# The sample cache on 128 partitions instead of 127, and four weight tiles queued later at the start

## The chip, the cores and the metric

The kernel runs on all 8 cores of one Trainium2 chip, each with its own part of the work and with no exchange between them. The time is that of the slowest core, in microseconds (us). The engines are named as in the profile: PE (TensorE, matmuls; PEld its weight loads), DVE (VectorE), ACT (ScalarE), POOL (GpSimd) and SP (SyncE, which here issues DMAs only). Each engine runs its own instructions strictly in the order in which they were written; semaphores join the engines.

## The reference

One inference step of a two-layer decoder trunk of width 1024, for 4 prompts of 4096 rows and for 128 samples of one row each. Layer 0 is a mixer with two halves (sliding-window attention over 128 positions with 8 heads, 2 key/value heads of 64, a relative-position bias and a sink; and a chunked gating network), layer 1 a gated recurrence. After each comes a feed-forward network of width 2816 with a residual.

What matters here is the attention of the samples. Each sample has a cache of the last 128 keys and values, and one new key and value:

```
k_all = concat(cache_k, k_new)                     # 129 positions
bias  = -inf where (distance < 0) or (distance >= 128), else rel_bias[bucket(distance)]
o     = softmax(q k_all / 8 + bias, with the sink) v_all
new_k_sample = k_all[1:]                           # the last 128 positions
```

The oldest cached row lies at distance 128, outside the window: it takes no part in the attention, and it is not in the returned cache either. So 127 of the 128 cached rows are used.

## The kernel before

A core has 18 blocks of 128 prompt rows and 16 samples. The blocks form four groups, A (blocks 0 to 3), B (4 to 8), C (9 to 12 and the samples) and D (13 to 17). Each group passes through layer 0's mixer (`l0`), its feed-forward network (`f0`), layer 1's mixer (`l1`) and its network (`f1`). The plan pairs them in nine phases, so that a mixer of one group runs beside a network of another; the samples' attention falls into phase 4, where `l0` of group C runs beside `f1` of group B.

The order of the work is not written by hand. Each operation is recorded with what it reads and writes, and a planner (`Sched`) gives every engine one fixed list. An operation's due time is its place in its phase, by the matmul time recorded before it, minus its `lead`. A DMA that opens a buffer, or that waits for nothing, is held back until the matmuls have come within 0.15 of its due time. The planner's costs decide the order only; at run time the lists are followed as they stand.

Two queues carry the loads. POOL issues the weights (`load_w`, L620: tiles of 128 x 2048, from fp32 to bf16 on the way, 512 KB as written), into 6 buffers `wm` for the mixers and 4 buffers `wf` for the networks. SP issues everything else. In the program's first phase POOL begins with six `wm` tiles: `kv`, `q0`, `q1`, `u0`, `u1`, `g0`. SP begins with a gain, a table, four blocks of rows (`X<-xin`, 512 KB each) and then small constants, `qkn` among them.

The samples' cache comes in four groups of four samples (`cache_group`, L849 on). For each group SP loads four samples' keys and then their values (L852) into fp32 tiles `p` of 127 partitions x 4 x 128: one cached row on each partition. ACT or POOL casts each tile to bf16 (L596), PE transposes the keys (L861), ACT or DVE copies the result, and the scores and sums follow later (`sample_group`). That is eight loads of 254 KB. In the traces such a tile is called `p`, as is every tile of that pool; `p<-ck` and `p<-cv` are the loads. Between the fourth and the fifth stands the load of a table, `gain<-lnr` (L1280).

The returned cache is moved by two copies in DRAM, `nks<-ck` and `nvs<-cv` (L1324), issued much earlier, and a store of the new row.

Of the kernel before, what the change touches and what calls it, by code (L numbers as in the profile page):

```python
# [9 lines left out]
ALU = mybir.AluOpType  # L10
AF = mybir.ActivationFunctionType
# [343 lines left out]
NS = 16  # L355
# [46 lines left out]
def _t5_bucket_np(dist):  # L402
    d = np.maximum(dist, 0)
    dl = np.maximum(d, 1).astype(np.float32)
    val = (np.log(dl / np.float32(16)) / np.float32(math.log(128 / 16)) * np.float32(16)).astype(np.float32)
    large = 16 + val.astype(np.int32)
    large = np.minimum(large, 31)
    return np.where(d < 16, d, large)


def build_consts():
    ohA = np.zeros((33, 384), np.float32)
    for j in range(384):
        dist = j - 128
        if 0 <= dist < 128:
            ohA[int(_t5_bucket_np(np.array(dist))), j] = 1.0
        else:
            ohA[32, j] = 1.0
    ohS = np.zeros((33, 128), np.float32)
    for j in range(128):  # L420
        ohS[int(_t5_bucket_np(np.array(127 - j))), j] = 1.0
    return ohA, ohS


# [59 lines left out]
def build_program(NG, WIDX):  # L484
    nc = bass.Bass("TRN2", target_bir_lowering=False)
    din = lambda name, shape: nc.dram_tensor(name, list(shape), F32, kind="ExternalInput").ap()
    dout = lambda name, shape: nc.dram_tensor(name, list(shape), F32, kind="ExternalOutput").ap()
    xin = din("xin", [NTOK + NS, D])
    ck_d = din("ck", [NS, 127, 128])
    cv_d = din("cv", [NS, 127, 128])  # L490
    sin_d = din("sin", [NS, 8, 128, 128])
    wall = din("wall", [NG, 128, 2048])
    par_d = din("par", [128, 22])
# [29 lines left out]
    with es:  # L523
        S = Sched()
        nsem = [0]

        def mksem():
            nsem[0] += 1
            return Sem(es.enter_context(nc.semaphore("d%d" % nsem[0])))

        def sb(name, shape, dt):
            return es.enter_context(nc.sbuf_tensor(name, list(shape), dt))

        def mkpool(name, n, size, dt, dma=False, **kw):
            t = sb(name, [128, n, size], dt)
            return Pool(name, [t[:, i, :] for i in range(n)], [mksem() for _ in range(n)] if dma else None, **kw)
# [3 lines left out]
        pWM = mkpool("wm", 6, 2048, BF16, dma=True, fifo=True, margin=0.4)  # L540
# [15 lines left out]
        identB = sb("identB", [128, 128], BF16)  # L556
# [4 lines left out]
        onesB = sb("onesB", [128, 64], BF16)  # L561
# [11 lines left out]
        biasS = sb("biasS", [128, 8], F32)  # L573
# [15 lines left out]
        def ra(st, bl, half):  # L589
            return [r_aT[(st.col[b] // 128, half)] for b in bl]  # L590
# [4 lines left out]
        def cp(e, out, in_):  # L595
            return e.copy(out=out, in_=in_) if CUR[0] == "act" else e.tensor_copy(out=out, in_=in_)  # L596
# [15 lines left out]
        outs = []  # L612
# [20 lines left out]
        r_id, r_mk, r_v1, r_par, r_rel, r_qn, r_ws, r_bs, r_bs0, r_bs1, r_ab, r_tab, r_es, r_pp, r_qk = [Buf("c%d" % i) for i in range(15)]  # L633
# [116 lines left out]
        def l0(st):  # L750
            g0 = load_gain(nrm_d[0])
            w_kv = load_w(pWM, "kv")
            w_q = [load_w(pWM, "q%d" % k) for k in range(2)]
            w_u = [load_w(pWM, "u%d" % c) for c in range(2)]
            w_g = [load_w(pWM, "g%d" % c) for c in range(2)]
            allb = st.kv + ([SB] if st.samples else [])
            norm(st, allb, g0)
            qT = {}
# [87 lines left out]
            def cache_group(q):  # L846
                n4 = slice(4 * q, 4 * q + 4)
                c3 = lambda ap: ap.rearrange("p (n f) -> p n f", n=4)
                cast = []  # L849
                for src in (ck_d, cv_d):  # L850
                    f = p25.get("cache", 2)
                    S.op("sp", lambda e, f=f, src=src: e.dma_start(out=c3(f.ap[0:127, 0:512]), in_=src[n4].rearrange("n j f -> j n f")), w=[f], dma=f, nbytes=1 << 19, lead=0.2)  # L852
                    c = p12.get("cacheb")
                    S.op(("act", "pool"), lambda e, f=f, c=c: cp(e, c.ap[0:127, 0:512], f.ap[0:127, 0:512]), r=[f], w=[c])
                    cast.append(c)
                kb, vb = cast
                kts, bt = p12.get("kts"), bank()

                def tr(e):
                    for j in range(4):  # L860
                        i = e.transpose(bt.bf[:, j * 128:j * 128 + 127], kb.ap[0:127, j * 128:(j + 1) * 128], identB[0:127, 0:127])  # L861
                    return i
                S.op("pe", tr, r=[kb, r_id], w=[bt])
                S.op(ANY, lambda e: cp(e, c3(kts.ap[:, 0:512])[:, :, 0:127], c3(bt.bf[:, 0:512])[:, :, 0:127]), r=[bt], w=[kts])
                return kts, vb

            def sample_group(kts, vb, vn, pd, qt, qp, q):
                bs = bank()

                def sc(e):  # L870
                    for j in range(4):
                        i = e.matmul(bs.ap[0:127, j * 8:(j + 1) * 8], lhsT=kts.ap[:, j * 128:j * 128 + 127], rhs=qp()[:, 4 * q + j, :], start=True, stop=True)
                    return i
                S.op("pe", sc, r=[kts, qt], w=[bs])
                f = p25.get("attS")
                S.op("dve", lambda e: e.tensor_tensor(out=f.ap[0:127, 0:32].rearrange("p (n h) -> p n h", n=4), in0=bs.ap[0:127, 0:32].rearrange("p (n h) -> p n h", n=4),
                                                      in1=biasS[0:127].unsqueeze(1).broadcast_to([127, 4, 8]), op=ALU.add), r=[bs, r_tab], w=[f])
                S.op("act", lambda e: e.activation(out=qt.ap[0:127, 128 + 32 * q:160 + 32 * q], in_=f.ap[0:127, 0:32], func=AF.Exp), r=[f], w=[qt])
                pt = lambda: qt.ap[0:127, 128 + 32 * q:160 + 32 * q].rearrange("p (n h) -> p n h", n=4)
                p3 = lambda: pd.ap[0:NS, 0:128].rearrange("p (n h) -> p n h", n=NS)  # L880
                bo = bank()

                def pv(e):
                    for g in range(2):
                        o = bo.ap[g * 64:(g + 1) * 64, 0:16]
                        for j in range(4):
                            e.matmul(o[:, j * 4:(j + 1) * 4], lhsT=vb.ap[0:127, j * 128 + g * 64:j * 128 + g * 64 + 64], rhs=pt()[:, j, 4 * g:4 * g + 4], start=(j == 0), stop=False, skip_group_check=True)
                        e.matmul(o.rearrange("p (n h) -> p n h", n=4), lhsT=vn.ap[0:NS, 128 + g * 64:192 + g * 64], rhs=p3()[:, 4 * q:4 * q + 4, 4 * g:4 * g + 4], start=False, stop=True, skip_group_check=True)
                    for g in range(2):
                        o = bo.ap[g * 64:(g + 1) * 64, 64:80].rearrange("p (n h) -> p n h", n=4)  # L890
                        e.matmul(o, lhsT=onesB[0:127, :], rhs=pt()[:, :, 4 * g:4 * g + 4], start=True, stop=False)
                        e.matmul(o, lhsT=onesB[0:NS, :], rhs=p3()[:, 4 * q:4 * q + 4, 4 * g:4 * g + 4], start=False, stop=False)
                        i = e.matmul(o, lhsT=onesB[0:1, :], rhs=es8[0:1, 4 * g:4 * g + 4].unsqueeze(1).broadcast_to([1, 4, 4]), start=False, stop=True)
                    return i
                S.op("pe", pv, r=[vb, vn, pd, qt, r_es, r_mk], w=[bo])
                S.op("dve", lambda e: e.reciprocal(out=f.ap[:, 32:48], in_=bo.ap[:, 64:80]), r=[bo], w=[f])
                c0 = st.sl(SB).start + 4 * q
                S.op("dve", lambda e: e.tensor_tensor(out=aTm[:, 0:4, c0:c0 + 4], in0=bo.ap[:, 0:16].rearrange("p (n c) -> p c n", c=4), in1=f.ap[:, 32:48].rearrange("p (n c) -> p c n", c=4), op=ALU.mult),
                     r=[bo, f], w=ra(st, [SB], 0))
# [383 lines left out]
        def at(phase, s):  # L1283
            S.key = (phase, s)
            stream[0] = s
# [35 lines left out]
                    ffn(st, int(what[1]), st.body if what == "f0" else st.out, 1 if what == "f0" else 3)  # L1321
        at(3, 0)
        for dst, src in ((nks_d, ck_d), (nvs_d, cv_d)):
            outs.append(S.op("sp", lambda e, dst=dst, src=src: e.dma_start(out=dst[:, 0:127, :], in_=src), dma=mksem(), nbytes=1 << 21))  # L1324
        at(9, 0)
        fin = S.op("sp", lambda e: e.nop())
        for o in outs:
# [85 lines left out]
```

How the kernel before makes its waits and increments, by code:

```python
    def emit(self, e, eng, sems):  # L330
        known = {}
        CUR[0] = e
        for o in self.q[e]:
            waits = {}
            for d in o.deps:
                if not self.needs_sync(o, d):
                    continue
                s = d.sem.sem if d.dma is not None else sems[d.eng]
                k = id(s)
                if known.get(k, 0) >= d.val:
                    continue
                if k not in waits or waits[k][1] < d.val:
                    waits[k] = (s, d.val)
            for k, (s, v) in waits.items():
                eng.wait_ge(s, v)
                known[k] = v
            ins = o.fn(eng)
            if o.dma is not None:
                ins.then_inc(o.sem.sem, 16)
            elif o.need_inc:
                ins.then_inc(sems[e], 1)
```

## Time and profile before

| | us |
|---|---|
| median of 2 runs (1962.88 and 1968.40) | 1965.64 |
| the profiled execution | 1965.01 |
| its span on core 3, the slowest | 1963.5 |
| shortest span of a core (core 6) | 1950.5 |
| PE busy, of the span | 1733.7 (88%) |
| DVE, ACT, POOL busy | 1112.3, 582.1, 449.3 |

The profile is of core 3. What lies around the span is 1.5 us. PE is busy for 88% of the span, and that share is an average over phases that differ. Idle time of an engine is put down to what ended it: "<-ACT p L596" means that an ACT instruction of line 596 that writes a tile `p` came last. A DMA appears twice: as the time in which its queue issues it (SPq), and as the time until it has landed.

### The profile page before, as it was taken

What the parts mean: (1) busy time and instruction counts of PE and PEld (TensorE: products, weight loads), DVE (VectorE), ACT (ScalarE), POOL (GpSimd) and SP (SyncE); (2) the same over time, 40 slices, a digit from 0 to 9 for tenths busy, and PEclk for the clock granted to TensorE, in tenths of its full rate; (3) what the DMA queues carried; (4) which work ended last, traced back from release to release, by engine and by line L of the source; (5) the groups of instructions that cost most, each with busy time, mean ns of one, the idle gap of its engine ahead of it and who ended that gap; (6) DMA issues with size and microseconds to landing.
All of it is one profiled execution on the core that took longest, in us unless ns stands there. A gap on an engine that the chain in (4) does not pass through costs nothing.

```text
span 1963.5 us, 36549 instructions; the slowest of 8 cores (1950.5 to 1963.5 us)
## 1 busy us (share of the span) xinstructions
PE 1733.7 (88%) x12194; PEld 1099.9 (56%) x12194; DVE 1112.3 (57%) x2374; ACT 582.1 (30%) x1130; POOL 449.3 (23%) x772
## 2 busy tenths in 40 slices
PE   3789988999988834699997999899989999989998
PEld 2355546665666422456565566566665676746565
DVE  3464555664677631354354455778674677766444
ACT  2334224431455221122113322433231353412111
POOL 3251131112222221122114122322221311212110
PEclk9789999999999977798998999999999999999999
DMA  9748889998679652574686588577876766836866
GB/s 193 170 90 137 141 155 189 156 155 149 121 130 150 114 90 51 118 126 77 127 149 157 96 149 154 95 159 162 175 153 124 112 108 99 132 57 124 147 115 144
DMA packets 107958, 257.68 MB, mean 131 GB/s; under 512 B 9030, under 2 KB 49936, under 8 KB 107744
## 3 DMA queue, kind: packets, MB, share of 16 engines
q0 software_dynamic: 57024, 203.45, 62.6%
q1 hardware_dynamic: 50752, 51.90, 8.8%
q8 instruction: 103, 1.69, 0.3%
q14 instruction: 79, 0.65, 0.1%
HBM read 440.91 MB, written 19.90 MB: 235 GB/s over the span
## 4 chain that ended last, share of the span: by engine, by line
PE 63%; DMA 11%; DVE 9%; SPq 6%; issue 5%; POOL 3%; ACT 2%; DVEq 0%; POOLq 0%; ACTq 0%
PE bank L1035 24%; PE bank L1053 16%; PE bank L731 7%; SPq L852 6%; PE bank L1089 5%; DMA wf<-wall 4%; PE bank L1120 2%; DMA p<-cv 2%; POOL st L630 2%; DMA X<-abuf 2%; PE bank L1266 1%; DMA qkn_sb<-qkn 1%; DVE Sst L1207 1%; PE bank L1165 1%; DMA X<-xin 1%
## 5 line engine op out<-in xcount | busy, mean ns | idle before, releaser
L1035 PE MATMUL bank<-hT,wf 128*128 128x320 bf16 (+3 forms) x4928 | 695.9, 297 | 34.9 <-ACT p L980 12.8
L1035 PEld LDWEIGHTS bank<-hT,wf 128*128 128x128 bf16 x4928 | 478.1, 99 | 211.5 <-issue 52.1
L1053 PE MATMUL bank<-wf,af 128*128 128x512 bf16 (+1 forms) x1540 | 353.3, 382 | 14.8 <-DVE af L1041 9.8
L620 POOL DMA_DIRECT2D wf<-wall x272 | 151.4, 558 | 780.9 <-PE bank L1035 488.4
L1039 ACT ACTIVATE ft<-bank 128x320 f32<-128x320 f32 (+3 forms) x308 | 130.0, 424 | 497.8 <-PE bank L1035 460.4
L1040 DVE SCALAR_TENSOR_TENSOR ft<-ft,bank 128x320 f32<-128x320 f32 (+3 forms) x308 | 144.0, 468 | 234.3 <-ACT ft L1039 233.8
L1053 PEld LDWEIGHTS bank<-wf,af 128*128 128x128 bf16 (+1 forms) x1540 | 147.2, 98 | 194.5 <-issue 31.8
L1058 DVE SCALAR_TENSOR_TENSOR X<-bank,X 128x512 f32<-128x512 f32 (+1 forms) x210 | 144.1, 689 | 157.8 <-PE bank L1053 154.8
L1041 DVE TENSOR_TENSOR af<-ft,bank 128x320 bf16<-128x320 f32 (+3 forms) x308 | 144.9, 470 | 66.8 <-PE bank L1035 30.4
L630 POOL TENSOR_TENSOR st<-st,mhalf 128x1 f32<-128x1 f32 (+5 forms) x165 | 145.5, 882 | 24.2 <-POOL st L629 0.2
L716 ACT ACTIVATE hb<-X 128x1024 bf16<-128x1024 f32 (+1 forms) x72 | 75.9, 1054 | 210.9 <-DVE X L744 122.8
L1089 PE MATMUL bank<-wm,hT 128*128 128x256 bf16 (+1 forms) x1120 | 133.7, 273 | 1.6 <-DVE aTm L601 0.9
L731 PE MATMUL bank<-wm,aTm 128*128 128x512 bf16 (+1 forms) x560 | 131.8, 383 | 0.3 <-issue 0.2
L620 POOL DMA_DIRECT2D wm<-wall x124 | 69.8, 566 | 269.6 <-PE bank L731 64.9
L629 POOL TENSOR_SCALAR st<-st 128x1 f32<-128x1 f32 (+5 forms) x165 | 45.2, 274 | 334.9 <-ACT hb L716 112.2
L1089 PEld LDWEIGHTS bank<-wm,hT 128*128 128x128 bf16 (+1 forms) x1120 | 107.0, 97 | 21.1 <-issue 5.9
L718 DVE SCALAR_TENSOR_TENSOR hb<-X,st,gain 128x1024 bf16<-128x1024 f32 (+1 forms) x72 | 91.9, 1283 | 36.4 <-POOL st L630 36.2
L731 PE MATMUL bank<-wm,hT 128*128 128x512 bf16 (+3 forms) x440 | 94.4, 371 | 13.7 <-ACT hT L596 12.6
L723 PE MATMUL bank<-identB,hb 128*128 128x128 bf16 (+1 forms) x576 | 46.1, 232 | 59.3 <-DVE hb L718 58.3
L731 PEld LDWEIGHTS bank<-wm,aTm 128*128 128x128 bf16 (+1 forms) x560 | 54.2, 98 | 64.5 <-issue 5.8
L744 DVE TENSOR_TENSOR X<-bank,X 128x512 f32<-128x512 f32 (+1 forms) x70 | 48.3, 690 | 65.0 <-PE bank L731 64.9
L723 PEld LDWEIGHTS bank<-identB,hb 128*128 128x128 bf16 (+1 forms) x576 | 38.2, 105 | 70.7 <-issue 68.3
(207 smaller groups left out, 1752.1 us busy)
## 6 DMA issues: line engine op xcount, KB each, us to landing
wf<-wall POOLq DMA_DIRECT2D x256, 512.0 KB, 7.8
wm<-wall POOLq DMA_DIRECT2D x124, 512.0 KB, 8.1
X<-xin SPq DMA_DIRECT2D x18, 512.0 KB, 19.4
gain<-nrm SPq DMA_DIRECT2D x16, 512.0 KB, 7.4
y<-X SPq DMA_DIRECT2D x16, 512.0 KB, 11.5
p<-sin SPq DMA_DIRECT2D x32, 256.0 KB, 8.2
sts<-p SPq DMA_DIRECT2D x32, 256.0 KB, 4.9
wf<-wall POOLq DMA_DIRECT2D x16, 256.0 KB, 5.4
```

The source lines that it names most:

```text
L620: S.op("pool", lambda e: e.dma_start(out=b.ap[:, 0:cols], in_=wall[g][:, 0:cols]), w=[b], dma=b, nbytes=nb * cols // 2048, lead=lead)
L630: S.op("pool", lambda e: e.tensor_tensor(out=st.ap[0:rw, o:o + n], in0=st.ap[0:rw, i:i + n], in1=mhalf[0:rw, 0:n], op=ALU.pow), r=[r_id], ...
L718: S.op("dve", lambda e, s=s, hb=hb, x=x, n=n: e.scalar_tensor_tensor(out=hb.ap[0:n], in0=x.ap[0:n], scalar=s.ap[0:n, 1:2], in1=gain.ap[0:n ...
L731: i = e.matmul(o(), lhsT=lhs[:, k, st.sl(blk)], rhs=wsel(k), start=(k == 0), stop=(k == nk - 1))
L852: S.op("sp", lambda e, f=f, src=src: e.dma_start(out=c3(f.ap[0:127, 0:512]), in_=src[n4].rearrange("n j f -> j n f")), w=[f], dma=f, nbyte ...
L1035: i = e.matmul(b.ap[:, 0:n], lhsT=w.ap[:, o + k * 128:o + k * 128 + 128], rhs=hT[st.par][:, k, lo:lo + n], start=(k == 0), stop=(k == 7))
L1039: S.op("act", lambda e, t=t, bg=bg, n=n: e.activation(out=t.ap[:, 0:n], in_=bg.ap[:, 0:n], func=AF.Tanh, scale=0.5), r=[bg], w=[t])
L1040: S.op("dve", lambda e, t=t, bg=bg, n=n: e.scalar_tensor_tensor(out=t.ap[:, 0:n], in0=t.ap[:, 0:n], scalar=1.0, in1=bg.ap[:, 0:n], op0=ALU ...
L1041: S.op("dve", lambda e, t=t, bu=bu, a=a, lo=lo, n=n: e.tensor_tensor(out=a.ap[:, lo:lo + n], in0=t.ap[:, 0:n], in1=bu.ap[:, 0:n], op=ALU.m ...
L1053: i = e.matmul(b.ap[0:n], lhsT=act[k].ap[:, st.sl(blk)], rhs=w[k // 4].ap[:, (k % 4) * 512:(k % 4) * 512 + 512], start=(k == 0), stop=(k = ...
L1058: S.op("dve", lambda e, b=b, n=n, xs=xs: e.scalar_tensor_tensor(out=xs(), in0=b.ap[0:n], scalar=0.5, in1=xs(), op0=ALU.mult, op1=ALU.add), ...
L1089: r = e.matmul(b.ap[0:n, i * 256:(i + 1) * 256], lhsT=hT[st.par][:, k, st.sl(blk)], rhs=w.ap[:, k * 256:(k + 1) * 256], start=(k == 0), st ...
```

## The change

The cache is handed over with all 128 rows, and each of the eight loads takes 128 partitions. All that follows in `cache_group` and `sample_group` takes 128 partitions too. The oldest row, now row 0, gets the bias that stands for "outside the window" (row 32 of the table, -30000), so that its exponential is zero. The copies of the returned cache leave row 0 out: 16 pieces of 127 rows as before, now with a gap in the source as well.

The second part is a `lead`. For group A alone the tiles `u0`, `u1` get a lead of -0.16 and `g0`, `g1` one of -0.18 instead of 0.3.

```diff
-        ohS[int(_t5_bucket_np(np.array(127 - j))), j] = 1.0
+        ohS[int(_t5_bucket_np(np.array(128 - j))) if j else 32, j] = 1.0
...
-    ck_d = din("ck", [NS, 127, 128])
-    cv_d = din("cv", [NS, 127, 128])
+    ck_d = din("ck", [NS, 128, 128])
+    cv_d = din("cv", [NS, 128, 128])
...
-            w_u = [load_w(pWM, "u%d" % c) for c in range(2)]
-            w_g = [load_w(pWM, "g%d" % c) for c in range(2)]
+            late = 0 in st.kv
+            w_u = [load_w(pWM, "u%d" % c, lead=-0.16 if late else 0.3) for c in range(2)]
+            w_g = [load_w(pWM, "g%d" % c, lead=-0.18 if late else 0.3) for c in range(2)]
...
-                    S.op("sp", lambda e, f=f, src=src: e.dma_start(out=c3(f.ap[0:127, 0:512]), in_=src[n4].rearrange("n j f -> j n f")), w=[f], dma=f, nbytes=1 << 19, lead=0.2)
+                    S.op("sp", lambda e, f=f, src=src: e.dma_start(out=c3(f.ap[0:128, 0:512]), in_=src[n4].rearrange("n j f -> j n f")), w=[f], dma=f, nbytes=1 << 19, lead=0.2)
                     c = p12.get("cacheb")
-                    S.op(("act", "pool"), lambda e, f=f, c=c: cp(e, c.ap[0:127, 0:512], f.ap[0:127, 0:512]), r=[f], w=[c])
+                    S.op(("act", "pool"), lambda e, f=f, c=c: cp(e, c.ap[0:128, 0:512], f.ap[0:128, 0:512]), r=[f], w=[c])
...
-            outs.append(S.op("sp", lambda e, dst=dst, src=src: e.dma_start(out=dst[:, 0:127, :], in_=src), dma=mksem(), nbytes=1 << 21))
+            outs.append(S.op("sp", lambda e, dst=dst, src=src: e.dma_start(out=dst[:, 0:127, :], in_=src[:, 1:128, :]), dma=mksem(), nbytes=1 << 21))
...
-            ck=np.ascontiguousarray(cache_k[0, c * NS:(c + 1) * NS, 1:].reshape(NS, 127, 128)),
-            cv=np.ascontiguousarray(cache_v[0, c * NS:(c + 1) * NS, 1:].reshape(NS, 127, 128)),
+            ck=np.ascontiguousarray(cache_k[0, c * NS:(c + 1) * NS].reshape(NS, 128, 128)),
+            cv=np.ascontiguousarray(cache_v[0, c * NS:(c + 1) * NS].reshape(NS, 128, 128)),
```

The instructions of PE, DVE, ACT and SP stand in the same order in both kernels; only shapes of 127 become 128. One engine's order differs, POOL's at the very start (`L629` and `L630` are the two steps of a block's norm). Before:

```order
L620 DMA wm<-wall 128x2048 x6
L697 AFFINE_SELECT identF<-identF 128x128
...
L629 TENSOR_SCALAR st<-st 128x1
L630 TENSOR_TENSOR st<-st,mhalf 128x1
L629 TENSOR_SCALAR st<-st 128x1
L630 TENSOR_TENSOR st<-st,mhalf 128x1
L629 TENSOR_SCALAR st<-st 128x1
L630 TENSOR_TENSOR st<-st,mhalf 128x1
L629 TENSOR_SCALAR st<-st 128x1
L630 TENSOR_TENSOR st<-st,mhalf 128x1
```

With the change:

```order
L620 DMA wm<-wall 128x2048 x3
L697 AFFINE_SELECT identF<-identF 128x128
...
L629 TENSOR_SCALAR st<-st 128x1
L630 TENSOR_TENSOR st<-st,mhalf 128x1
L629 TENSOR_SCALAR st<-st 128x1
L630 TENSOR_TENSOR st<-st,mhalf 128x1
L629 TENSOR_SCALAR st<-st 128x1
L630 TENSOR_TENSOR st<-st,mhalf 128x1
L620 DMA wm<-wall 128x2048 x3
L629 TENSOR_SCALAR st<-st 128x1
L630 TENSOR_TENSOR st<-st,mhalf 128x1
```

Three of the six tiles (`u0`, `u1`, `g0`) moved behind the norm of the third block of rows.

ACT's list around the cache's casts, which keeps its places, reads with the change (numbered lines above 754 are one higher than before):

```order
L596 COPY p<-bank 128x512
L596 CAST p<-p 128x512 x2
L1040 ACTIVATE ft<-bank 128x256
L596 COPY hT<-bank 128x8x128
...
L596 CAST p<-p 128x512 x2
L596 CAST vt<-bank 128x2x64
L981 ACTIVATE p<-bank 128x512 x3
L596 CAST p<-p 128x512
L981 ACTIVATE p<-bank 128x512
L1040 ACTIVATE ft<-bank 128x320 x9
```

Five of the eight casts stand on ACT, each ahead of work for the running prompt blocks: the copy of normed rows (`hT`), the values (`vt`), the exponentials (`L981`) and the network's activations (`L1040`).

## Rows read from the trace of the kernel before

**Rows 1.** Span and mean granted clock, by core.

```profile
core 3: 1963.5 us, clock 0.953
...
core 6: 1950.5 us, clock 0.955
```

**Rows 2.** The page: busy tenths of PE in 40 slices of the span.

```profile
PE   3789988999988834699997999899989999989998
```

**Rows 3.** What ended PE's idle time, 700 to 810 us: total, times, longest.

```profile
PE bank L861 <- ACT p L596: 17.7, 1, 17.7
PE bank L974 <- ACT vt L596: 13.1, 1, 13.1
PE bank L1035 <- ACT p L980: 12.8, 1, 12.8
PE bank L731 <- ACT hT L596: 10.8, 1, 10.8
PE bank L861 <- POOL p L596: 5.9, 1, 5.9
```

**Rows 4.** SP's queue in order of time: start, duration, line, what.

```profile
661.39 40.60 SPq L852 DMA_DIRECT2D p<-ck  x1
...
767.44 12.02 SPq L852 DMA_DIRECT2D p<-cv  x1
...
797.24 0.87 SPq L615 DMA_DIRECT2D y<-X  x2
801.17 1.56 SPq L708 DMA_DIRECT2D X<-xin  x2
```

**Rows 5.** ACT in order of time, end of the same stretch.

```profile
770.62 0.62 ACT L596 CAST p<-p 127x512 bf16<-127x512 f32 x1 [15.53 <-DMA p<-cv]
...
799.78 0.62 ACT L596 CAST p<-p 127x512 bf16<-127x512 f32 x1 [26.41 <-DMA p<-cv]
```

**Rows 6.** POOL in the same stretch: one of the eight casts.

```profile
782.61 0.61 POOL L596 CAST p<-p 127x512 bf16<-127x512 f32 x1 [25.39 <-DMA p<-ck]
```

**Rows 7.** Stretches: length, busy by engine, granted clock, DMA share, GB/s.

```profile
710.00:800.00 90.00, 30.71 (x151) 16.54 (x150) 10.57 (x21) 7.81 (x17) 8.65 (x11) 0.63 0.25 61
801.00:826.00 25.00, 24.80 (x168) 17.03 (x168) 10.93 (x22) 6.66 (x15) 4.34 (x9) 0.90 0.60 112
1060.00:1110.00 50.00, 47.99 (x342) 28.15 (x340) 27.89 (x67) 22.28 (x44) 19.03 (x24) 0.98 0.46 78
```

**Rows 8.** Stretch in which hardly anything but a cache load moves.

```profile
760.00:780.00 20.00, 5.92 (x21) 2.19 (x21) 2.03 (x4) 2.37 (x5) 0.00 (x0) 0.66 0.08 22
```

**Rows 9.** DMA issues: KB each, median us to landing.

```profile
p<-sin SPq DMA_DIRECT2D x32, 256.0 KB, 8.2
...
gain<-lnr SPq DMA_DIRECT2D x3, 512.0 KB, 17.6
```

**Rows 10.** PE before the stretch and in it.

```profile
690.94 1.91 PE L1035 MATMUL bank<-hT,wf 128*128 128x256 bf16 x16 [0.24 <-DMA wf<-wall]
...
728.10 3.33 PE L1035 MATMUL bank<-hT,wf 128*128 128x256 bf16 x16
```

**Rows 11.** DVE: last norm row of the stage before the stretch.

```profile
704.93 1.54 DVE L718 SCALAR_TENSOR_TENSOR hb<-X,st,gain 128x1024 bf16<-128x1024 f32 x1 [0.53 <-POOL st L630]
```

**Rows 12.** Chain that ended last, start of the program: start, length, what.

```profile
5.04 26.31 DMA qkn_sb<-qkn
...
45.80 30.49 DMA X<-abuf
```

**Rows 13.** Stretches of the start, columns as in Rows 7.

```profile
0.00:30.00 30.00, 3.89 (x24) 2.57 (x24) 5.65 (x16) 6.94 (x11) 9.41 (x29) 1.00 0.95 205
30.00:40.00 10.00, 6.53 (x34) 4.01 (x35) 5.51 (x12) 1.56 (x3) 4.03 (x6) 1.00 0.76 147
40.00:70.00 30.00, 23.00 (x135) 12.13 (x133) 12.86 (x30) 10.18 (x23) 13.04 (x18) 0.92 1.01 187
```

**Rows 14.** POOL at the start.

```profile
24.20 0.57 POOL L630 TENSOR_TENSOR st<-st,mhalf 128x1 f32<-128x1 f32 x1
```

More of the change, by code:

```diff
@@ L860, in tr @@
                     for j in range(4):
-                        i = e.transpose(bt.bf[:, j * 128:j * 128 + 127], kb.ap[0:127, j * 128:(j + 1) * 128], identB[0:127, 0:127])
+                        i = e.transpose(bt.bf[:, j * 128:j * 128 + 128], kb.ap[0:128, j * 128:(j + 1) * 128], identB[0:128, 0:128])
                     return i
                 S.op("pe", tr, r=[kb, r_id], w=[bt])
-                S.op(ANY, lambda e: cp(e, c3(kts.ap[:, 0:512])[:, :, 0:127], c3(bt.bf[:, 0:512])[:, :, 0:127]), r=[bt], w=[kts])
+                S.op(ANY, lambda e: cp(e, c3(kts.ap[:, 0:512])[:, :, 0:128], c3(bt.bf[:, 0:512])[:, :, 0:128]), r=[bt], w=[kts])
                 return kts, vb
@@ L871, in sc @@
                     for j in range(4):
-                        i = e.matmul(bs.ap[0:127, j * 8:(j + 1) * 8], lhsT=kts.ap[:, j * 128:j * 128 + 127], rhs=qp()[:, 4 * q + j, :], start=True, stop=True)
+                        i = e.matmul(bs.ap[0:128, j * 8:(j + 1) * 8], lhsT=kts.ap[:, j * 128:j * 128 + 128], rhs=qp()[:, 4 * q + j, :], start=True, stop=True)
                     return i
@@ L875, in sample_group @@
                 f = p25.get("attS")
[L876 to L879, printed above, removed]
+                S.op("dve", lambda e: e.tensor_tensor(out=f.ap[0:128, 0:32].rearrange("p (n h) -> p n h", n=4), in0=bs.ap[0:128, 0:32].rearrange("p (n h) -> p n h", n=4),
+                                                      in1=biasS[0:128].unsqueeze(1).broadcast_to([128, 4, 8]), op=ALU.add), r=[bs, r_tab], w=[f])
+                S.op("act", lambda e: e.activation(out=qt.ap[0:128, 128 + 32 * q:160 + 32 * q], in_=f.ap[0:128, 0:32], func=AF.Exp), r=[f], w=[qt])
+                pt = lambda: qt.ap[0:128, 128 + 32 * q:160 + 32 * q].rearrange("p (n h) -> p n h", n=4)
                 p3 = lambda: pd.ap[0:NS, 0:128].rearrange("p (n h) -> p n h", n=NS)
@@ L886, in pv @@
                         for j in range(4):
-                            e.matmul(o[:, j * 4:(j + 1) * 4], lhsT=vb.ap[0:127, j * 128 + g * 64:j * 128 + g * 64 + 64], rhs=pt()[:, j, 4 * g:4 * g + 4], start=(j == 0), stop=False, skip_group_check=True)
+                            e.matmul(o[:, j * 4:(j + 1) * 4], lhsT=vb.ap[0:128, j * 128 + g * 64:j * 128 + g * 64 + 64], rhs=pt()[:, j, 4 * g:4 * g + 4], start=(j == 0), stop=False, skip_group_check=True)
                         e.matmul(o.rearrange("p (n h) -> p n h", n=4), lhsT=vn.ap[0:NS, 128 + g * 64:192 + g * 64], rhs=p3()[:, 4 * q:4 * q + 4, 4 * g:4 * g + 4], start=False, stop=True, skip_group_check=True)
@@ L890, in pv @@
                         o = bo.ap[g * 64:(g + 1) * 64, 64:80].rearrange("p (n h) -> p n h", n=4)
-                        e.matmul(o, lhsT=onesB[0:127, :], rhs=pt()[:, :, 4 * g:4 * g + 4], start=True, stop=False)
+                        e.matmul(o, lhsT=onesB[0:128, :], rhs=pt()[:, :, 4 * g:4 * g + 4], start=True, stop=False)
                         e.matmul(o, lhsT=onesB[0:NS, :], rhs=p3()[:, 4 * q:4 * q + 4, 4 * g:4 * g + 4], start=False, stop=False)
```

## The prediction

> **What bounds the kernel now.** I read the spans first: core 3 is the slowest, at an ordinary clock [rows 1]. Then the row of 40 slices, of 49.1 us each: PE is busy for nine tenths or so almost everywhere, with one long hole, slices 15 to 17 (3, 4 and 6 tenths), or 687 to 835 us [rows 2]. So outside this hole a change has to shorten PE's own chain, and inside it whatever PE waits for. A second, shorter hole is slice 1, the start.
>
> In the hole, five waits of PE make 17.7 + 13.1 + 12.8 + 10.8 + 5.9 = 60.3 us [rows 3]. One is for a cast on POOL, the others for something on ACT. Neither engine is short of time: in 710 to 800 us ACT is busy for 7.81 us of 90 and POOL for 8.65 [rows 7]. They stand still because their lists are followed in order and the next item is a cast of a cache tile: the casts waited 15.53, 26.41 and 25.39 us for their DMA [rows 5, 6]. Behind each cast on ACT stands work of the prompt blocks, and that is how a load for 16 samples stops the whole core.
>
> Why are the loads late? SP holds one load of the cache for 40.60 us and another for 12.02 [rows 4]; SP seems to be blocked by what is ahead of it. While hardly anything but such loads moves, the transfers run at 22 GB/s with a DMA share of 0.08, about one engine of sixteen (0.0625) [rows 8]. The last casts confirm the size: a tile landed for the cast at 782.61 us, 12.0 us after that at 770.62, and 254 KB in 12.0 us is 21.7 GB/s [rows 5, 6]. Eight such loads need at least 96 us in series. The loads `p<-sin` have the same layout, also runs of 512 B and nearly the same bytes, on 128 partitions, and land after 8.2 us with much else in flight [rows 9]. So short runs are not the reason, and 127 partitions are what differs.
>
> **The change, part by part.**
>
> *The eight loads.* Each gets 256 KB instead of 254. The nearest row gives 8.2 us to landing, the other end is today's 12 us in series [rows 9, 5, 6]. I take 8.2, because `p<-sin` agrees in layout, direction and queue. The first four loads then land while PE is still busy, before 700 us. The table `gain<-lnr` stands behind them in SP's queue and needs a buffer that the last norm of the running network reads, which ends at 704.93 + 1.54 = 706.5 us [rows 11]. So the last four loads are issued at about 707 to 709 and land by about 718. When are they wanted? The third value tile's cast was met at 770.62 - 15.53 = 755.1 us and the last one at 799.78 - 26.41 = 773.4 [rows 5]. Ahead of the first lie waits of 17.7 + 10.8 = 28.5 us, ahead of the second also the 13.1 [rows 3]: without them the casts are met at 727 and 732. All eight are in time, with some 9 us to spare at the tightest place, less what the clock gives back.
>
> *What is left of the hole.* PE's order is unchanged, so the work of 710 to 800 us stays: 30.71 us of PE time at a mean granted clock of 0.63 [rows 7]. Part of it ran at the lower of the two clock levels, 1.2 GHz instead of 2.4: 16 matmuls of 256 columns took 3.33 us there and 1.91 us before the hole [rows 10]. If all of it stayed as it is, 30.7 us would remain; if it all scaled with the mean clock, 30.71 x 0.63 = 19.3. I take 27 us, nearer to the upper end: the low clock lay mostly on time in which PE did nothing, and the first microseconds will still run low, since PE is sparse just ahead of the hole. The same kind of stage of group D, without samples, shows PE busy for 47.99 us of 50 [rows 7]; here the chain is thinner, so I allow 10% of waits and get 30 us for 90. That saves 60 us. Ends: 56 (30.7 us and 10% of waits) and 71 (19.3 us and none).
>
> *After the hole.* From 801 to 826 us the clock is 0.90 although PE is busy for 24.80 us of 25 [rows 7]: the engine comes out of a wait and starts low. Without the wait some 25 x 0.10 = 2.5 us come back. What is late next? The stores `y<-X` and the loads `X<-xin` that followed the cache loads in SP's queue (797.24 and 801.17) [rows 4] move forward with it, so they are no new wait. The weights were held up by PE, not the other way round: a DMA share of 0.25 in the hole and 0.60 behind it leave room [rows 7]. So nothing is given back: 60 + 2.5 = 62.5 us.
>
> *The work on 128 partitions.* Casts, transposes, copies and sums stay as many as they were. By proportion each takes at most 128/127 of its time; at 0.62 us for a cast [rows 5] some forty of them are under 0.3 us, which the other engines' work hides. The two copies in DRAM stay 16 pieces of the same size, and I cost them at nothing: no engine waits for them before the end. If they fell on one engine as the cache loads did, weights would share that engine for a while; they did so in the hole, and no wait of PE there names a weight [rows 3].
>
> *The weights at the start.* The chain starts with DMAs: `qkn` from 5.04 us on for 26.31 us, behind rows and weights, and then `X<-abuf` from 45.80 us on for 30.49 [rows 12]. The change takes three tiles of 512 KB (1.5 MB) out of the first rush, and issues them after the third block's norm, which ends at 24.20 + 0.57 = 24.8 us [rows 14]. At the 205 GB/s of the first 30 us, 1.5 MB are 7.7 us [rows 13]. At best the constants land that much earlier and everything shifts by 7.7 us. At worst the late tiles hold up the next step instead: `X<-abuf` lies in a stretch with a DMA share of 1.01 [rows 13], and the 1.5 MB now fall nearer to it. What surely can be won is idle DMA time, and there is 0.24 x 10 = 2.4 us of it in 30 to 40 us [rows 13]. I take 2.5 us, with ends of -7 (the tiles are late for PE) and +7.7.
>
> Here a rule of the Trainium skill speaks against the change. The rows show a DMA share of 0.95 and 1.01 around that gap [rows 13]. The page "DMA: Bandwidth & Descriptors", section "Issuing engines are not separate DMA queues", says that DMAs of SP and POOL run on the same 16 engines and interleave. By that rule a new order of the same bytes wins nothing as long as all of them are needed, and the sum would end at 62.5 us rather than 65.
>
> **Sum.** 62.5 + 2.5 = 65 us, from the profiled execution's 1965.0 us (its span and 1.5 us around it): 1900 us. The median of the runs shown is 1965.6, so against it that is 3.3% less. All cores run this program; the slowest one before carries the stall in full, and I take it for the slowest after.
>
> **The rivals.**
>
> A. The forecast: the hole closes and the start gains a little. 1900, by the ends above (56 + 2.5 - 7 to 71 + 2.5 + 7.7, not all at once) 1885 to 1913. Chance 0.55.
>
> B. The hole closes, and the start gains nothing or loses: the 1.5 MB only move from one queue of bytes to another. For it speaks the saturated DMA on both sides [rows 13], against it that `qkn` sits behind those bytes in the chain [rows 12]. 1902 to 1909, say 1903. Chance 0.25.
>
> C. A wait takes the place of the one removed: the last four loads, held behind `gain<-lnr` until 706.5 us, come too late. That table took 17.6 us to landing [rows 9]. If the four land one after another behind it, the last one lands at 706.5 + 17.6 + 4 x 8.2 = 757 us, 25 us after ACT meets its cast. 1900 + 25 = 1925. Against it: those 17.6 us were measured behind the slow loads. Chance 0.11.
>
> D. The change does not do what it says: 128 partitions are still moved by one engine, and `p<-sin` is quick for another reason. Then the hole stays, and the time is 1963. Against it stands the row of `p<-sin`. By the skill's page just named, section "Why a DMA increments its semaphore by 16 and not by 1", a load runs on the largest number of engines up to 16 that divides the outer size on both sides: one for 127, sixteen for 128. The trace agrees on 127 with its 22 GB/s; by that page D is out. Chance 0.05.
>
> E. Slower than before: the cache now has steps of 64 KB between the four samples of a load, where 127 rows made 63.5 KB. If runs at such steps get in each other's way in DRAM, each load may take longer than today's 12 us, and that is the point from which it decides: at twice that, the eight take 96 us more. 1965 + 96 = 2061. Against it: the four runs of `p<-sin` lie 8 x 128 x 128 x 4 B = 512 KB apart, a power of two as well, and it lands in 8.2 us [rows 9]. Chance 0.04.
>
> **Numbers.** A and B hold 0.80 and reach from 1885 to 1913; with the cases of C in which the loads are only a little late, the range is 1885 to 1917. A measurement of this kernel tells about 2% (39 us, so 1926) from no change. Faster by more: A, B and most of C, 0.89. Within 2%: D and the rest of C, 0.07. Slower: E, 0.04.
>
> **What would show it.** In the changed profile the loads `p<-ck` and `p<-cv` should have an issue time under 1 us each and land in under 10 us; the waits of L861, L974 and L1035 on ACT and POOL should be gone from the list, and the hole's stretch should be some 30 us long. If C is right, SP issues the table at about 706 us and casts still wait after it. At the start, the tile `qkn` should land before 31 us, and the second `X<-abuf` tells whether that was worth anything: before 74 us for A, at 76 for B. The forecast is wrong if PE's waits reappear under another name in 700 to 830 us, for weights above all, or if the clock stays low after the stretch.

## The result, and the profile after

| | before | changed |
|---|---|---|
| median, us | 1965.64 | 1902.76 (1899.50 and 1906.02) |
| ratio, 95% interval | | 0.968 [0.959, 0.977] |
| profiled execution, us | 1965.01 | 1899.50 |
| its span, slowest core | 1963.5 (core 3) | 1897.9 (core 2) |

The forecast was 1900. In some executions the cores of one half of the chip run at a lower clock; the ratios leave these executions out, so that in a few comparisons below a median over all of them lies apart from its ratio.

Span and clock of the slowest and the quickest core, answering to [rows 1]:

```profile
core 2: 1897.9 us, clock 0.963
...
core 4: 1880.8 us, clock 0.972
```

The page's row of PE's busy tenths, 40 slices, of 47.4 us now [rows 2]. Slices 14 to 16, 617 to 759 us, show 7, 8 and 8, and the hole of three slices is gone:

```profile
PE   4589988899989788999979999899989999989998
```

SP's queue (start, duration, line, what; numbered lines above 754 are one higher than before) [rows 4]. Each cache load holds SP for 0.37 to 0.50 us, where one held it for 40.60. The table `gain<-lnr` waits for its buffer until 712.96 us, and the last four loads follow within 2 us:

```profile
646.82 0.38 SPq L853 DMA_DIRECT2D p<-ck  x1
...
712.96 0.34 SPq L1281 DMA_DIRECT2D gain<-lnr  x1
713.40 0.37 SPq L853 DMA_DIRECT2D p<-ck  x1
...
714.92 0.50 SPq L853 DMA_DIRECT2D p<-cv  x1
...
739.00 1.60 SPq L615 DMA_DIRECT2D y<-X  x2
741.78 6.42 SPq L708 DMA_DIRECT2D X<-xin  x2
```

DMA issues: KB each, median us to landing [rows 9]. The cache loads land after 5.9 and 6.5 us, a little quicker than `p<-sin`, the row that stood for them. The table between them, `gain<-lnr`, lands after 9.2 us instead of 17.6. The two copies in DRAM took 24.4 and 28.4 us before:

```profile
p<-sin SPq DMA_DIRECT2D x32, 256.0 KB, 7.4
...
gain<-lnr SPq DMA_DIRECT2D x3, 512.0 KB, 9.2
X<-abuf SPq DMA_DIRECT2D x2, 512.0 KB, 36.5
p<-ck SPq DMA_DIRECT2D x4, 256.0 KB, 5.9
p<-cv SPq DMA_DIRECT2D x4, 256.0 KB, 6.5
nks<-ck SPq DMA_DIRECT2D x1, 1016.0 KB, 25.8
nvs<-cv SPq DMA_DIRECT2D x1, 1016.0 KB, 30.3
```

ACT and POOL in order of time, the casts [rows 5, 6]. None has a DMA behind its name any more:

```profile
714.99 1.14 ACT L596 CAST p<-p 128x512 bf16<-128x512 f32 x2
...
731.26 1.14 ACT L596 CAST p<-p 128x512 bf16<-128x512 f32 x2
...
736.86 0.62 ACT L596 CAST p<-p 128x512 bf16<-128x512 f32 x1 [0.32 <-PE bank L976]
```

```profile
733.99 0.60 POOL L596 CAST p<-p 128x512 bf16<-128x512 f32 x1
```

What ended PE's idle time, 700 to 760 us (total, times, longest) [rows 3]. Of the five waits of 60.3 us only that of L731 is still there, with 1.5 us; the longest left are the two of a norm, and a weight makes 0.4 us:

```profile
PE bank L723 <- DVE hb L718: 2.7, 2, 1.6
PE bank L731 <- ACT hT L596: 1.5, 1, 1.5
...
PE bank L1036 <- DMA wf<-wall: 0.4, 1, 0.4
```

PE in order of time, first of the kernel before (core 3), then of the changed one (core 2). The same transposes open both (L1000, now L1001) and the same long run of the network closes both (L1035, now L1036):

```profile
709.45 0.58 PE L1000 MATMUL bank<-identB,p 128*128 128x128 bf16 x4 [1.40 <-DVE p L994]
...
801.04 9.14 PE L1035 MATMUL bank<-hT,wf 128*128 128x320 bf16 x48 [12.83 <-ACT p L980]
```

```profile
699.79 3.37 PE L1036 MATMUL bank<-hT,wf 128*128 128x256 bf16 x16
...
715.92 0.59 PE L1001 MATMUL bank<-identB,p 128*128 128x128 bf16 x4 [1.50 <-DVE p L995]
...
739.42 5.87 PE L1036 MATMUL bank<-hT,wf 128*128 128x320 bf16 x42
```

Before, 801.04 - 709.45 = 91.6 us lie between the two; now 739.42 - 715.92 = 23.5. And that stretch and the 25 us after it, columns as in [rows 7]:

```profile
715.92:739.42 23.50, 21.67 (x137) 13.39 (x140) 9.77 (x20) 7.50 (x16) 6.85 (x8) 0.90 0.55 108
739.42:764.42 25.00, 24.62 (x187) 17.58 (x184) 11.56 (x22) 7.47 (x16) 5.52 (x11) 1.00 0.88 192
```

PE is busy for 21.67 us where it took 30.71 in the 90 us of [rows 7], at a granted clock of 0.90 instead of 0.63, and the 25 us after it run at 1.00 instead of 0.90.

**The start** gained nothing on the slowest cores; in the row of tenths above, its hole got deeper (slice 2, 47 to 95 us, shows 5 where it showed 7 [rows 2]). Chain of the start (start, length, what) [rows 12], and stretches of it [rows 13] with one behind it:

```profile
34.06 5.98 DMA abuf<-p
...
40.55 39.46 DMA X<-abuf
```

```profile
30.00:40.00 10.00, 9.72 (x59) 5.41 (x59) 5.93 (x14) 4.33 (x11) 5.42 (x9) 1.00 1.00 176
40.00:70.00 30.00, 13.96 (x80) 6.79 (x79) 8.43 (x20) 7.36 (x15) 10.48 (x14) 0.77 0.97 167
80.00:130.00 50.00, 40.41 (x221) 19.61 (x226) 27.59 (x56) 19.57 (x34) 15.27 (x24) 0.67 0.47 105
```

The table load `X<-abuf` is issued 5.2 us earlier than before (40.55 instead of 45.80) and lands 3.7 us later (80.0 instead of 76.3). POOL's DMAs at that time:

```profile
26.92 1.71 POOL L620 DMA_DIRECT2D wm<-wall  x3
...
31.65 2.22 POOL L620 DMA_DIRECT2D wf<-wall  x4
...
35.58 0.54 POOL L620 DMA_DIRECT2D wm<-wall  x1 [1.72 <-PE bank L675]
```

The three tiles of the change are followed, 5 us later, by four tiles `wf`, the first weights of the network, and these by `g1`, the seventh tile of the first block. The first reader of the `wf` tiles, of 138 matmuls up to 200 us (count; ns min/median/max; first and last start):

```profile
L1036 PE MATMUL bank<-hT,wf x138: 323/326/326, 139.5 to 200.0; 128*128 128x384 bf16 x138
```

So 2 MB are queued at 31.65 us that nobody reads before 139.5, and two things that are read much sooner stand behind them: `g1` and `X<-abuf`. PE in order of time, before and then changed. L909 (now L910) reads `u0` and `u1`; the L731 behind it (its 128x512 form) reads `g0` and `g1`:

```profile
47.28 1.46 PE L909 MATMUL bank<-hT,wm 128*128 128x384 bf16 x8
...
56.86 5.34 PE L731 MATMUL bank<-wm,hT 128*128 128x512 bf16 x24
```

```profile
40.12 1.46 PE L910 MATMUL bank<-hT,wm 128*128 128x384 bf16 x8
...
61.91 6.74 PE L731 MATMUL bank<-wm,hT 128*128 128x512 bf16 x23 [12.05 <-DMA wm<-wall]
```

PE came to these weights 7.2 us earlier and then stood still for 12.05 us until a `wm` tile had landed. The trace does not tell tiles of one pool apart; by its place in the queue, and by the longest landing of a `wm` tile in this stretch, 25.8 us (35.58 + 0.54 + 25.8 = 61.9), it is `g1`. For `X<-abuf`, which the chain names, PE waited another 2.9 us, in two waits. The means of the eight cores say the same: L910 starts at 40.0 us instead of 47.2, the wait for the tile is 10.2 us instead of 2.4, and the L731 behind it starts at 59.9 instead of 59.7. The whole 7.2 us were gone at that tile; the waits for `X<-abuf` came to 2.3 us instead of 4.1.

### The profile page after: what moved, and what is told of

Read it like the earlier page. It is cut to its first block, busy times and chain, and to the rows that moved or that the text cites. A ratio compares the mean times of both kernels' runs of the same rounds, so it can differ in the third digit from the quotient of the medians.

```text
span 1897.9 us, 36455 instructions; the slowest of 8 cores (1880.8 to 1897.9 us)
## 1 busy us (share of the span) xinstructions
PE 1713.1 (90%) x12100; PEld 1096.7 (58%) x12194; DVE 1112.7 (59%) x2374; ACT 582.5 (31%) x1130; POOL 451.4 (24%) x772
## 4 chain that ended last, share of the span: by engine, by line
PE 68%; DVE 10%; DMA 9%; issue 6%; POOL 3%; ACT 2%; DVEq 0%; SPq 0%; POOLq 0%; ACTq 0%
PE bank L1036 25%; PE bank L1054 16%; PE bank L731 9%; PE bank L1090 4%; DMA wf<-wall 3%; DMA X<-xin 2%; PE bank L1121 2%; DMA X<-abuf 2%; POOL st L630 2%; PE bank L1267 1%; PE bank L1166 1%; PE bank L975 1%; DVE Sst L1208 1%; PE bank L976 1%; PE bank L723 1%
## 5 line engine op out<-in xcount | busy, mean ns | idle before, releaser
L1036 PE MATMUL bank<-hT,wf 128*128 128x320 bf16 (+3 forms) x4928 | 692.5, 296 | 23.6 <-DMA wf<-wall 12.7
L1036 PEld LDWEIGHTS bank<-hT,wf 128*128 128x128 bf16 x4928 | 477.3, 99 | 196.5 <-issue 38.9
L1054 PE MATMUL bank<-wf,af 128*128 128x512 bf16 (+1 forms) x1493 | 347.2, 383 | 17.4 <-DVE af L1042 7.1
L1040 ACT ACTIVATE ft<-bank 128x320 f32<-128x320 f32 (+3 forms) x308 | 130.0, 424 | 499.1 <-PE bank L1036 457.7
L1054 PEld LDWEIGHTS bank<-wf,af 128*128 128x128 bf16 (+1 forms) x1540 | 147.5, 98 | 191.6 <-issue 29.7
L630 POOL TENSOR_TENSOR st<-st,mhalf 128x1 f32<-128x1 f32 (+5 forms) x165 | 145.8, 884 | 24.2 <-POOL st L629 0.2
L731 PE MATMUL bank<-wm,aTm 128*128 128x512 bf16 (+1 forms) x540 | 128.8, 382 | 1.7 <-issue 0.8
L629 POOL TENSOR_SCALAR st<-st 128x1 f32<-128x1 f32 (+5 forms) x165 | 45.9, 278 | 331.6 <-ACT hb L716 112.7
L731 PE MATMUL bank<-wm,hT 128*128 128x512 bf16 (+3 forms) x422 | 88.9, 361 | 17.3 <-DMA wm<-wall 12.1
L731 PEld LDWEIGHTS bank<-wm,aTm 128*128 128x128 bf16 (+1 forms) x560 | 54.1, 98 | 64.1 <-issue 5.0
```

What stands on the lines that cost most here:

```text
L630: S.op("pool", lambda e: e.tensor_tensor(out=st.ap[0:rw, o:o + n], in0=st.ap[0:rw, i:i + n], in1=mhalf[0:rw, 0:n], op=ALU.pow), r=[r_id], ...
L731: i = e.matmul(o(), lhsT=lhs[:, k, st.sl(blk)], rhs=wsel(k), start=(k == 0), stop=(k == nk - 1))
L1036: i = e.matmul(b.ap[:, 0:n], lhsT=w.ap[:, o + k * 128:o + k * 128 + 128], rhs=hT[st.par][:, k, lo:lo + n], start=(k == 0), stop=(k == 7))
L1040: S.op("act", lambda e, t=t, bg=bg, n=n: e.activation(out=t.ap[:, 0:n], in_=bg.ap[:, 0:n], func=AF.Tanh, scale=0.5), r=[bg], w=[t])
L1054: i = e.matmul(b.ap[0:n], lhsT=act[k].ap[:, st.sl(blk)], rhs=w[k // 4].ap[:, (k % 4) * 512:(k % 4) * 512 + 512], start=(k == 0), stop=(k = ...
```

## The experiments

Theory: (1) a load from SP's queue runs on as many DMA engines as the partition count allows, one for 127, and the slow loads alone make the hole; (2) the reordered weights only change places among bytes that are needed anyway, and gain nothing. Rivals: an odd count is the trouble, or the number of bytes; and the change's two parts gain only together.

**Either part alone, and the whole again** (one chip, same runs of before):

> The change with its second part undone: the cache on 128 partitions, all six weight tiles issued at once at the start. Theory 1 (the whole gain is the closed hole, the moved tiles give nothing): same time as the changed kernel, 1902 us within 3; the stretch from the first cache load to the long run of matmuls behind the hole takes about 92 us instead of 157, and the second table load of the start lands at 71 to 79 us as before. Theory 2 (the moved tiles give the 2.5 us of the forecast): 1905 us. Theory 3 (the moved tiles cost what the start lost in the changed profile): 1899 us.

> The kernel before with the second part alone: three of six weight tiles issued behind the third block's norm, the cache still on 127 partitions. Theory 1 (bytes only change places): 1965 us within 3, although the constants land some 5 us earlier and the table store is issued 5 us earlier on every core; the second table load lands at 73 to 80 us all the same, since the four network tiles are still ahead of it. Theory 2 (the start gains): 1963 us or less, the second table load before 74 us on most cores.

> The changed kernel once more, on the same chip as the two parts, to compare with them: 1902 us within 4 by every theory.

Edits: for the first the leads put back, for the second the kernel before with the leads alone:

```diff
-            w_u = [load_w(pWM, "u%d" % c) for c in range(2)]
-            w_g = [load_w(pWM, "g%d" % c) for c in range(2)]
+            w_u = [load_w(pWM, "u%d" % c, lead=-0.16 if 0 in st.kv else 0.3) for c in range(2)]
+            w_g = [load_w(pWM, "g%d" % c, lead=-0.18 if 0 in st.kv else 0.3) for c in range(2)]
```

| kernel | median, us | ratio to before |
|---|---|---|
| cache part alone | 1898.64 | 0.9672 [0.9652, 0.9692] |
| leads alone | 1972.56 | 1.0016 [0.9985, 1.0047] |
| both | 1902.62 | 0.9692 [0.9652, 0.9733] |

The cache part is the whole gain that can be measured. The leads are worth nothing that can be told from noise. Alone they change the time by -0.15 to +0.47%, and the 2.5 us of the sum would be -0.13%, just inside the interval's end. On top of the cache part, 1902.62 against 1898.64 us is what was expected if they cost something, but the two intervals overlap.

**The partition count.** The kernel before, with fewer of the 127 rows loaded and used, so that the attention leaves 14, 5, 3 or 6 cached rows out. For 113 (with 122, 124 and 121 in the others; the casts, transposes and sums follow):

```diff
-                    S.op("sp", lambda e, f=f, src=src: e.dma_start(out=c3(f.ap[0:127, 0:512]), in_=src[n4].rearrange("n j f -> j n f")), ...
+                    S.op("sp", lambda e, f=f, src=src: e.dma_start(out=c3(f.ap[0:113, 0:512]), in_=src[n4, 0:113].rearrange("n j f -> j n f")), ...
```

> The same with 113 rows, a prime (14 rows left out). Theory (one engine, as for 127): loads of 226 KB at 22 GB/s, 10.7 us each instead of 12; the hole stays and shrinks only by the bytes, 8 x 1.3 = 10 us: about 1953 us. Rival (the bytes or the number of runs count, not the divisor): between the times of 112-odd and 121 rows, below 1910 us.

> The kernel before with 122 rows of each cache loaded and used instead of 127 (5 rows of the attention are left out). Theory (a load runs on the largest number of engines up to 16 that divides its partitions; 122 = 2 x 61, so two): 44 GB/s, about 5.7 us for a load instead of 12; the first four are in time, the last four still late by some 5 to 15 us in all, so the hole loses most of its 60 us of waits: about 1912 us. Rival (any number but 128 is slow): 1963 us.

> The same with 124 rows (3 rows left out). Theory (124 = 4 x 31, so four engines): 88 GB/s, about 3 us a load, quick enough to be hidden: no wait for a cast, about 1903 us. Rival (any number but 128 is slow): 1963 us.

> The same with 121 rows, an odd number below 122 (6 rows left out). Theory (121 = 11 x 11, so eleven engines): the loads are as quick as with 128, no wait for a cast, about 1903 us; faster than with 122 although the number is odd. Rival (any number but 128, or any odd one, is slow): 1963 us.

One execution of each:

| rows | largest divisor up to 16 | profiled execution, us | GB/s while a load runs nearly alone | longest hold of SP by a load, us |
|---|---|---|---|---|
| 127 (before) | 1 | 1964.32 | 22 [rows 8] | 40.60 [rows 4] |
| 113 | 1 | 1950.38 | 23 | 36.52 |
| 122 | 2 | 1921.44 | 41 | 10.89 |
| 124 | 4 | 1901.62 | 84 | 4.87 |
| 121 | 11 | 1898.12 | (no such stretch) | 2.07 |

The three rates come from these rows, columns as in [rows 7], first of 113, then of 122, then of 124 rows; the DMA share goes 0.08, 0.14, 0.28, near 1, 2 and 4 sixteenths:

```profile
735.00:742.00 7.00, 5.12 (x21) 2.63 (x22) 1.53 (x4) 2.61 (x5) 0.00 (x0) 0.65 0.08 23
```

```profile
664.00:669.00 5.00, 3.75 (x19) 1.98 (x20) 2.62 (x7) 2.88 (x6) 1.36 (x4) 0.59 0.14 41
```

```profile
665.00:669.00 4.00, 2.88 (x17) 1.21 (x15) 3.08 (x6) 1.06 (x2) 3.06 (x7) 1.00 0.28 84
```

What ended PE's idle time, 700 to 800 us, with 113 rows and with 122. With 113 the five waits of [rows 3] are all there and shorter (45.7 us, against 60.3); with 122 two are left, 12.9 us:

```profile
PE bank L1035 <- ACT p L980: 12.0, 1, 12.0
PE bank L974 <- ACT vt L596: 11.7, 1, 11.7
PE bank L731 <- ACT hT L596: 9.9, 1, 9.9
PE bank L861 <- ACT p L596: 7.6, 1, 7.6
PE bank L861 <- POOL p L596: 4.5, 1, 4.5
```

```profile
PE bank L1035 <- ACT p L980: 9.0, 1, 9.0
PE bank L861 <- POOL p L596: 3.9, 1, 3.9
```

With 121 rows, an odd number and fewer bytes than 122, the load with the longest hold of SP:

```profile
708.87 2.07 SPq L852 DMA_DIRECT2D p<-cv  x1
```

So neither odd counts nor bytes decide: 121 is quick, and 113, with the fewest bytes, is slow. The order is that of the largest divisor. The size for 122 was missed (9 us over the forecast). On its slowest core the first cache load is issued at 655.30 us, 8.5 later than in the changed kernel, which the loads don't explain, since they begin there. By the Trainium skill, page "DMA: Bandwidth & Descriptors", section "Why a DMA increments its semaphore by 16 and not by 1", a load runs on the largest number up to 16 that divides the outer sizes of both sides. These four runs agree with it at 1, 2 and 4 by their rates, at 11 by its time alone.

**The bytes ahead of `X<-abuf`.** The changed kernel, with the network's first four tiles issued when they are due and not before:

```diff
-                    w = load_w(pWF, "gu%d_%d" % (layer, j))
+                    w = load_w(pWF, "gu%d_%d" % (layer, j), lead=0.0 if 0 in st.kv and layer == 0 and j < 4 else 0.3)
```

> The changed kernel, and the first four tiles of the network's weights (2 MB) get a lead of 0 instead of 0.3: POOL issues them behind the start's last matmuls, at about 107 us, not at about 31. Theory 1 (the table load of the start waits for the bytes that POOL queued ahead of it): 2 MB at 190 GB/s are 11 us, so the second table load lands at 66 to 70 us instead of 73 to 80 and the kernel takes about 1894 us, unless the network's first matmuls, at about 130 us, then wait for their weights. Rival (SP's own rows and the short runs of the table are the limit, not POOL's queue): the table lands at 75 us or later and the time stays at 1902 us, or grows by what the network waits.

It took 1880.64 us, a ratio of 0.9578 [0.9558, 0.9599]: faster than both kernels, and by more than the forecast of some 1894, which gave the 2 MB 11 us. POOL and PE in order of time, then the stretches of its start (columns as in [rows 7]), then the landing of `X<-abuf`, on its slowest core:

```profile
88.75 2.14 POOL L620 DMA_DIRECT2D wf<-wall  x4
```

```profile
117.23 1.46 PE L1036 MATMUL bank<-hT,wf 128*128 128x384 bf16 x8
```

```profile
40.00:70.00 30.00, 21.87 (x122) 10.66 (x120) 13.76 (x29) 8.02 (x17) 11.99 (x17) 0.89 0.90 203
80.00:130.00 50.00, 42.12 (x296) 25.59 (x295) 33.43 (x60) 19.72 (x40) 29.27 (x40) 0.90 0.88 148
```

```profile
X<-abuf SPq DMA_DIRECT2D x2, 512.0 KB, 13.8
```

The tiles go out at 88.75 us and are in time for their first reader at 117.23, which waits for no DMA. `X<-abuf` lands after 13.8 us instead of 36.5, and PE runs on: 21.87 us busy in 40 to 70 us instead of 13.96. Neither wait is left: on none of the eight cores does PE wait for a `wm` tile or for `X<-abuf` there. In 80 to 130 us the granted clock is 0.90 instead of 0.67 on the slowest core. It is 0.90 on all eight cores here; in the changed kernel it goes from 0.67 on core 2, the slowest, to 0.93 on core 4, the quickest.

Then the same without the change's second part (the six tiles of the first block at once again), with a repeat of the run above beside it, and with two of the four tiles late (`j in (2, 3)`):

> The changed kernel's cache part and the four late network tiles, but without the second part of the change: the six weight tiles of the first block are queued at once again. Theory: the 1.5 MB of weights only change their place among bytes that are all needed before the first long run of PE, so their order is worth under 5 us either way: 1876 to 1886, within 0.3% of the next run. Rival: with the four network tiles out of the way the second part of the change does gain what it was given as a bound in the sum, up to 7.7 us, and this kernel is that much slower than the next: 1886 to 1889.

> The changed kernel with the four network tiles issued late, once more beside the one before it, on the same chip: 1877 to 1884 by both theories.

> The changed kernel with two of the four first network tiles (1 MB of the 2 MB) issued late, the other two as in the changed kernel. Theory: each byte queued ahead of the load X<-abuf costs it time in proportion, so half of the gain comes: the second group of L672 starts at about (77.7 + 62) / 2 = 70 us, mean of the cores, and the time is about (1902.6 + 1881) / 2 = 1892. Rival: it isn't the bytes but that any tile of that kind stands in POOL's queue ahead of the later ones; then one half brings nothing (77 us, 1902) or, if the queue was only too full for four, all of it (62 us, 1881).

The place to compare is the last matmul of L672, which reads the second table (means of the 8 cores, one execution each; `abuf<-p` is the store that opens `X<-abuf`, the wait is that of the L731 behind L909 or L910, and the cache column is the issue of the first cache load):

| kernel | store `abuf<-p` | PE's wait for a `wm` tile | `X<-abuf` to landing | last L672 starts | first cache load | ratio of times |
|---|---|---|---|---|---|---|
| before | 40.2 | 2.4 | 29.7 | 81.0 | 639.1 | 1 |
| leads alone | 33.7 | 9.2 | 34.4 | 79.0 | 636.2 | 1.0016 |
| cache part alone | 41.3 | 2.6 | 29.7 | 82.4 | 639.6 | 0.9672 |
| both (the change) | 33.6 | 10.2 | 34.8 | 79.8 | 638.3 | 0.9680 |
| the same again | 33.7 | 8.7 | 34.1 | 78.9 | 639.6 | 0.9692 |
| both, 2 of 4 tiles late | 33.1 | 2.9 | 28.1 | 72.5 | 631.9 | 0.9617 |
| cache part, 4 tiles late | 41.1 | 0 | 12.6 | 73.7 | 633.2 | 0.9618 |
| both, 4 tiles late | 33.9 | 0 | 12.3 | 66.7 | 622.3 | 0.9578 |
| the same again | 34.2 | 0 | 11.2 | 67.5 | 623.7 | 0.9553 |

My theory that the order of the first six tiles is worth under 5 us was wrong here: the kernel without the leads took 1891.54 us, over the 1876 to 1886 of the theory and the 1886 to 1889 of its rival. With the network's tiles out of the way the leads are worth 73.7 - 67.1 = 6.6 us at L672 and 0.9618 - 0.9553 = 0.65% of the time, some 13 us. The intervals, [0.9593, 0.9642] and [0.9523, 0.9582], don't touch; that of the earlier run of the quicker kernel reaches 0.9599 and just does. With those tiles in the way it is 2.0 to 3.5 us at L672 and nothing in the time. Half the tiles late bring about half of the way (72.5 between 79 to 80 and 67.1), so the cost grows with what is queued ahead and is not that of one tile's place in a list. Bytes and number of loads are not told apart, as all these tiles have the same size. This kernel ran on another chip, where the one before took 1985.36 us, so its forecast of 1892 us can't be compared; its ratio of 0.9617 [0.9561, 0.9673] lies between as well, with an interval too wide to say more.

## Why the prediction was right, and where it was not

**The time was right, its parts were not all.** On the slowest cores the 65.6 us of span split so: the start -3.5 (first cache load at 643.29 before, 646.82 now; over all cores' means it is +0.8), the hole 65.2 (from there to the long run of L1035: 157.75 before, 92.60 now), the rest 4.0 (1162.5 and 1158.5). The sum had 2.5, 60 and 2.5. That the total came out within 1 us of the forecast's 65 is luck: the hole gave 5.2 us more, the rest 1.5 more and the start 6.0 less.

- *The eight loads*: taken at 8.2 us to landing, they took 5.9 and 6.5, and the casts were met with all data there. The table ahead of the last four was issued at 712.96 us instead of some 707, as the norm it waited for came later; the casts behind, forecast for 727 and 732, ran at 731.26 and 736.86, so the room stayed. Shown by the counts 113 to 124 as well: the divisor of the count decides, and not the odd count, the bytes or the runs of 512 B, which all these loads have. That it is the number of DMA engines in use rests on the rates and shares for one, two and four.
- *What is left of the hole*: this term was mis-sized. 30 us were to remain of the 90; 23.5 remain of 91.6. PE's own time was 21.7 instead of 27, at a granted clock of 0.90 (27 lay nearer to the 30.7 of the 0.63 before than to the 19.3 of the full clock), and the waits were 1.8 us instead of 3. Ahead of it 2.9 us were lost (643.29 to 709.45 before, 646.82 to 715.92 now): 16 matmuls took 3.37 us there that took 1.91 before [rows 10], and the mean granted clock of that stretch was 0.86, against 0.90.
- *After the hole*: 4.0 us instead of 2.5, and nothing given back. No wait took the place of the old ones (rival C): the loads behind `gain<-lnr` were issued at 713.40 to 714.92, the third value cast ran at 731.26 without waiting.
- *Rivals D and E*: D, that one engine would still carry 128 rows, fell with the landing times. E, that steps of 64 KB hurt, fell too: the loads got quicker, and the copies in DRAM went from 24.4 and 28.4 to 25.8 and 30.3 us, which no engine waited for.
- *The start*: here the step failed. "What surely can be won is idle DMA time, and there is 0.24 x 10 = 2.4 us of it": the share of that gap did rise, from 0.76 to 1.00, but with the four network tiles, which POOL's list brought forward along with everything else (31.65 instead of 36.22 us), and not with bytes that somebody waited for. Both ends of that term came true, one after the other, where 2.5 us had been taken as a middle. Of the best case, +7.7, PE had 7.2 us when it came to L910: `qkn` landed at 26.4 us instead of 31.4 (slowest cores), and the store followed 6.6 us earlier (means). Then came the worst case, "the tiles are late for PE": behind the 2 MB the next `wm` tile was late, and PE waited 10.2 us for it instead of 2.4. `X<-abuf`, which the forecast named as the place to look, took 5.1 us longer (29.7 to 34.8, means), but PE's waits for it got shorter. Rival B was right on this part. Its reason, that the same bytes only change places, holds as long as the 2 MB lie among them; without them the same leads gave some 13 us.

The rule of the Trainium skill that spoke against this part ("DMA: Bandwidth & Descriptors", section "Issuing engines are not separate DMA queues": DMAs of SP and POOL run on the same 16 engines and interleave) agrees with these runs: tiles of POOL's queue delayed a load of SP's by some 22 us. What I drew from it, that a new order wins nothing, was too wide: it wins when the bytes put behind are not needed soon.

What stays open: the kernel with the four late tiles gains 13.1 us on the change at L672, 16.0 at the first cache load, 15.3 in the mean span of its cores (1889.2 to 1873.9) and 22 in the median of the slowest ones (1902.62 to 1880.64). The clock in 80 to 130 us, 0.67 to 0.93 over the cores of the one and 0.90 on every core of the other, would fit both the 3 us behind L672 and a larger gain of the slowest cores; no run took this apart.

## What to carry to other kernels

A load that is issued from SP and is slow without anything else moving deserves a look at its partition count before its bytes: if the DMA share is near 1/16, 2/16 or 4/16 (here 0.08, 0.14 and 0.28), pad the outer count to a multiple of 16 and mask the extra row, as was done here from 127 to 128. Look then at which in-order list stands behind the load's consumer, for that, not the 256 KB, made 60 us. And at the start of a program order all loads by first use, across the queues and within each: a prefetch for later costs what it delays, and what a reordering wins can be lost at the next tile behind it. To see where, look at PE's waits in order of time; the chain that ended last named only `X<-abuf` here.

## What was not expected

SP, which only issues, was held by one load of 127 rows for up to 40.60 us, and by one of 122 rows for 10.89, so a slow load delays the issue of what follows it, and not only its own data. A long hold alone is no sign of few engines, though: at the start of the changed kernel five loads `X<-xin` hold SP for 34.27 us, in a stretch with a DMA share of 0.97. 2 MB queued on POOL stretched two loads of 512 KB on SP from 12 to 34 us and made PE wait 10 us for a tile of POOL's own queue. And the change's second part, worth nothing measurable by itself, is worth some 0.65% of the time once the network's tiles make room.
